# Identity products ahead of the waits for normed chunks, in a two-block network kernel

## The reference, cut to what matters

```python
x = x + 0.5 * swiglu(rmsnorm(x, ffn1_norm), w_gate, w_up, w_down)      # width 2816
x = x + hybrid_mixer(rmsnorm(x, mix_norm), ...)                        # mix_w_in first
x = x + memory_cross_attention(rmsnorm(x, mem_q_norm), ...)            # queries from w_q
x = x + 0.5 * swiglu(rmsnorm(x, ffn2_norm), ...)
...                                                                    # final norm, RWKV-7 time mix
x = x + squared_relu_mlp(rms_norm(x, ln_mlp[0]), w1, w2)               # width 4096
k_sh, v_sh = shared_kv(x, kv_norm, w_kv, k_gain)
x = x + swa_layer(rms_norm(x, ln_mix[1]), k_sh, v_sh, ...)
x = x + squared_relu_mlp(rms_norm(x, ln_mlp[1]), w1, w2)
```

## Time and profile before

| | us |
|---|---|
| runs of the kernel (3) | 1727.09, 1718.46, 1713.05 |
| median | 1718.46 |
| profiled execution, its own time | 1726.43 |
| its span, first to last instruction | 1725.1 |
| mean granted clock of TensorE | 0.908 |

### The profile page before, as it was taken

One profiled execution on the slowest core, in us unless ns is written; L12 is line 12 of the kernel. 1 busy time (PEld: TensorE's weight loads), 2 busy tenths in 40 slices (PEclk: granted clock), 3 DMA queues, 4 the chain that ended last, 5 costly groups with the idle time before them and its releaser, 6 DMA issues. The chain is left out here.

```text
span 1725.1 us, 27799 instructions
## 1 busy us (share of the span) xinstructions
PE 1542.1 (89%) x12196; PEld 1468.8 (85%) x12196; DVE 993.1 (58%) x1277; ACT 698.9 (41%) x1058; POOL 48.7 (3%) x40
## 2 busy tenths in 40 slices
PE   8999999999799799999799632977999988799999
PEld 8999998787699799999797322877999987699999
DVE  5655653457564446555554679336666654756665
ACT  5444442244454344444354301223444443444443
POOL 0000000000200000000000010000000010000000
PEclk9999998899899989999799555797999978989999
DMA  7555452420345045555152000003454531035552
GB/s 269 188 188 186 166 183 94 171 99 1 132 162 189 32 147 176 192 189 188 66 181 88 24 1 1 26 1 122 171 176 180 183 116 55 6 143 196 196 183 87
DMA packets 33025, 222.26 MB, mean 129 GB/s; under 512 B 3887, under 2 KB 5167, under 8 KB 6536
## 3 DMA queue, kind: packets, MB, share of 16 engines
q1 hardware_dynamic: 31848, 219.42, 35.4%
q10 hardware_dynamic: 1056, 1.07, 0.2%
HBM read 219.40 MB, written 1.06 MB: 128 GB/s over the span
## 5 line engine op out<-in xcount | busy, mean ns | idle before, releaser
L304 DVE TENSOR_TENSOR tile_lo<-ring,tile_hi 128x1024 fp32r<-128x1024 f32 x396 | 479.3, 1228 | 429.2 <-ACT tile_hi L294 429.2
L294 ACT ACTIVATE tile_hi<-ring 128x1024 fp32r<-128x1024 f32 x396 | 409.0, 1052 | 352.5 <-PE ps L346 306.3
L344 PE MATMUL ps<-hT_hi,tile_hi 128*128 128x256 f32 x1600 | 460.7, 288 | 14.0 <-DVE hT_lo L506 13.3
L345 PE MATMUL ps<-hT_lo,tile_hi 128*128 128x256 f32 x1600 | 457.0, 286 | 0.0
L346 PE MATMUL ps<-hT_hi,tile_lo 128*128 128x256 f32 x1600 | 456.5, 285 | 0.0
L344 PEld LDWEIGHTS ps<-hT_hi,tile_hi 128*128 128x128 f32 x1600 | 310.4, 194 | 18.8 <-DVE hT_lo L506 14.1
L345 PEld LDWEIGHTS ps<-hT_lo,tile_hi 128*128 128x128 f32 x1600 | 310.4, 194 | 0.0
L346 PEld LDWEIGHTS ps<-hT_hi,tile_lo 128*128 128x128 f32 x1600 | 310.4, 194 | 0.0
L346 PE MATMUL ps<-hidden_hi,tile_lo 128*128 128x256 f32 x864 | 243.2, 281 | 0.0
L345 PE MATMUL ps<-hidden_lo,tile_hi 128*128 128x256 f32 x864 | 243.0, 281 | 0.0
L344 PE MATMUL ps<-hidden_hi,tile_hi 128*128 128x256 f32 x864 | 243.0, 281 | 0.0
(11 more groups left out here) (435 smaller groups left out, 2391.7 us busy)
## 6 DMA issues: line engine op xcount, KB each, us to landing
ring<-stream SPq DMA_DIRECT2D x204, 1024.0 KB, 4.8
x_sb<-x SPq DMA_DIRECT2D x4, 256.0 KB, 4.0
bias<-f_dram ACTq DMA_DIRECT2D x1, 1024.0 KB, 8.4
squares<-mem SPq DMA_DIRECT2D x1, 1024.0 KB, 4.8
cum<-rows SPq DMA_DIRECT2D x1, 1024.0 KB
out<-x_sb SPq DMA_DIRECT2D x4, 256.0 KB, 2.0
small_sb<-small SPq DMA_DIRECT2D x1, 485.5 KB, 8.9
const_sb<-const SPq DMA_DIRECT2D x1, 385.0 KB, 8.9
```

The source lines that it names most:

```text
L294: act.activation(e.w_hi[:, n % SPLIT, :], e.ring[:, tile % RING, span(n % 2, HALF)], ACT.Copy).then_inc(e.tile_hi.handle, 1)
L304: dve.tensor_tensor(e.w_lo[:, n % SPLIT, :], e.ring[:, CUT[n // 2] % RING, span(n % 2, HALF)], e.w_hi[:, n % SPLIT, :].bitcast(F32), ALU.s ...
L344: pe.matmul(out, left[0], right[0], start=start, stop=False)
L345: pe.matmul(out, left[0], right[1], start=False, stop=False)
```

## The change

Ahead of the wait for the second, third and fourth pair of chunks PE issues twelve identity products into bank 3. The first pair's wait is as before. No other engine's program changes. Bank 3 isn't in use at these points.

```diff
 def x_arrives(e, pe, k):
     if k % 2 == 0:
+        if k:
+            keep_busy(e, pe, 12, 3)
         pe.wait_ge(*e.sig("x_ready").since(k // 2 + 1))
```

## The result

The change costs 0.8%: 1732.58 us (median of 9 runs) against 1718.46 us before (9 runs), a ratio of 1.0076 with a 95% interval of 1.0049 to 1.0102, which is +8.4 to +17.5 us and clear of no change. The forecast was 1729.7 us and +0.65%. The profiled execution took 1732.58 us with a span of 1731.3 us, 6.2 us more than the one before.

A forecast was written before the change was run, and what follows sets the result against it. PE was taken to bound the kernel; 16.1 + 1.4 - 6.3 = +11.2 us on the profiled 1726.43 gives 1737.6, carried over to the 1718.46 median as 1729.7 us (+0.65%), range 1718 to 1744.

The forecast's parts named there:

- The price of a group: Twelve identity products leave 24 records and hold PE for 2.68 us at full clock, even when the pair is ready.
- (a): ffn1 and memq, with no wait to hide in: each pays three groups, +8.04 us, together +16.1 us.
- (b): Short waits in mix, ffn2, mlp1, mlp2: regained clock is spent on surplus products, 14.6 us to the spread, together +1.4 us.
- (c): Long wait in kv: with groups and full clock 17.9 us instead of 22.4, query products save 1.8, in all -6.3 us.
- The uncertain step: In kv, the 48 value products would hold the full clock, taking 5.66 us; no row showed whether they would.
- The sum: Over all seven places: 16.1 + 1.4 - 6.3 = +11.2 us against the profiled execution's 1726.43 us.
- third rival: At the short waits, ordinary runs' clock falls less often before the change; two places without falls give +19.8 us; chance 12%.
- The first: Rival: the clock falls at the waiting places in spite of the products, +45 us, 1763 us; chance 5%.
- The second: Rival: kv's value products lose the clock, so kv gains only 2.0 us; +15.5 us, 1734 us; chance 30%.
- The fourth: Rival: each product leaves one record, so a group costs 1.34 us everywhere; -10.5 us, 1708 us; chance 5%.
- The transposition rule: Trainium skill's rule that transpose-mode identity products don't engage full clock; carried over, the clock would fall as before; set aside.

The follow-up runs named there:

- e1_uncovered: Kernel before with groups of twelve identity products only in ffn1 and memq, where nothing waits: 1739.27 us against 1724.15, ratio 1.0085.
- e3_fitted: Kernel before with groups cut to the waits (6, 8, 0 in mix, ffn2, mlp1, mlp2; 5, 3, 17 in kv): 1695.64 us, ratio 0.9841.
- e4_one_column: e2_waits_only with filler products of one moving column instead of 128, same weights: 1779.12 us in one run, kernel before 1724.15.
- e2_waits_only: Kernel before with groups of twelve only in mix, ffn2, mlp1, kv and mlp2, where PE waits: 1714.95 us against 1724.15, ratio 0.9959.
- e9_transposes12: e2_waits_only with the identity transposed in place of multiplied, twelve at a time: 1708.65 us in one run.
- e10_half: Kernel before with smaller groups (3, 4, 0 in mix, ffn2, mlp1, mlp2; 3, 2, 8 in kv): 1706.36 us against 1721.83, ratio 0.9922.
- e6_transposes: e3_fitted with the identity transposed in place of multiplied, same counts: 1695.70 us in one run.
- e8_late_squares: Kernel before with groups only in kv (5, 3, 4), POOL's square additions after the fourth x_ready, column sums after the second half: 1709.30 us, ratio 0.9942.

## Why the prediction was right

**The price of a group.** Forecast 2.68 us, from one row of 24 records. In the trace after, a group begins at 1538.28 and the next pair's product starts at 1540.88; 2.60 us, and from group to group it is 3.39 us, which less the pair's 0.71 is 2.68. In memq and ffn1 nothing else came with it.

**(a) ffn1 and memq.** Forecast +8.04 each; measured +8.06 and +8.05, and e1_uncovered showed that they alone bring +14.7 us (+9 to +20) in the runs. This is where the change loses.

**(b) The four short waits.** Forecast 14.56 us, called 14.6, against 13.9 to 14.6 before; measured 14.67 to 14.70. The sum is +1.7 us where I had +1.4. That the clock was bought back, and that the products that outlast the waits cost the same again, is shown from both sides: by e3_fitted, which keeps the clock and drops the surplus (10.5 us), and by e4_one_column, which keeps the surplus and loses the clock (24.2 us). The 10.3 us that I reckoned for mlp2 without surplus and at full clock came out as 10.5.

**(c) kv.** Forecast 17.9 us to the first query product and -6.3 in all; it took 1424.02 - 1406.42 = 17.6 us, so -4.8, and -1.8 for the query products, -6.6. The 0.3 us are the value products: 0.112 us each at full clock, where I had taken the 0.118 of the wider ones. The uncertain step, that the value products would keep the clock, held in the change, e2_waits_only and e3_fitted; they lost it in e9_transposes12 and e10_half. PE stood 1.9 us before pair 3 in both, but 1.8 us in e6_transposes too, where they kept it, so the idle time alone doesn't tell the cases apart.

**The sum.** The places give 16.1 + 1.7 - 6.6 = +11.2 us, as forecast. That it agrees to the tenth is luck: +0.3 in (b) and -0.3 in (c) cancel. The medians of the runs lie 14.1 us apart, and the interval of 8.4 to 17.5 holds the forecast. What makes the other 2 to 3 us, if they are real, isn't settled. A candidate is the third rival in a mild form: in e1_uncovered's execution the places without groups took 13.25 to 13.92 us instead of 13.86 to 14.63, so the loss that the change removes may often be smaller than in the execution I read. But e2_waits_only, whose -7.1 us is more than the -4.9 of its places, points the other way. One judgement was off: I held a difference under 1% to be past telling, and with nine runs of each kernel 0.8% was told from none.

**The rivals.** The first (the clock falls anyway) didn't occur; e4_one_column shows a filling with which it does. The second (kv's value products lose the clock) didn't occur here but did with the smaller groups of e10_half. The third (falls are rarer in ordinary runs) isn't settled; in the one other profile without groups in these places, e1_uncovered, the clock fell in all five. The fourth (one record's time for each product) is false for products and true for transpositions, 12 records in 1.47 us. The transposition rule, which I had set aside because of the load stage's rows, was rightly set aside.

## What to carry to other kernels

Filler products on PE have a price that can be read off one row and a worth that is the clock alone; count them against the idle time of each place, and give none to a place that doesn't wait, even if it runs through the same helper. Here the same idea cost some 13 us with twelve everywhere and won some 27 with fitted ones, 14 in each of four places and 25 in the fifth. Fewer held the clock in most places, but not in all. Before filling a wait, look at what makes it: here it was another engine's work beside DVE's.

## What the runs showed that I hadn't expected

- Transposing the identity costs half of multiplying it: 12 records in 1.47 us against 24 in 2.84.
- POOL's additions beside DVE stretch both. L506 took up to 1.5 us in place of 0.48 (the six of them 5.52 against 2.46 us), and in e8_late_squares the two weight remainders that ran beside POOL took 3.89 us, where one alone takes 1.23. POOL's three additions took 5.73 us there, where the shortest in that trace took 1.27.
- The clock stayed at 0.50 for 20 us with PE busy 20.30 of 20.30 us, most of that time with one-column products.
- e3_fitted's four runs lie within 1.1 us of each other (1695.23 to 1696.30), those of the kernel before on the same chip within 13.9 us (1714.82 to 1728.67). The falls of the clock at the stage starts are hardly what makes that spread: e2_waits_only and the change held the clock there in their profiled executions, and their runs spread over 12.1 and 14.4 us.
